# A tenth 2 MB weight buffer in shared rooms, with the norm rows spread by products of depth one

## What is computed

```
probs = softmax(h @ router_w + router_b)          # 32 experts in 8 groups of 4
expert, wts = the 2 best experts of the best group, per token
hid = silu(xt @ w_gate[e]) * (xt @ w_up[e])       # 1024 -> 512
y   = hid @ w_down[e]                             # 512 -> 1024
out = sum over the token's two experts of wts * y
x   = layer_norm(ALPHA * x + out, ln_g[i, 1], ln_b[i, 1])
```

## Time and profile before

| | |
|---|---|
| median of 3 runs | 1246.2 us (1245.13 to 1247.28) |
| profiled execution: span | 1245.5 us |
| TensorE busy | 1028.4 us, 83% of the span |
| VectorE, ScalarE, GpSimd busy | 24%, 15%, 3% |
| DMA | 451.10 MB, mean 362 GB/s |
| SP's queue | 442.51 MB, 86.0% of 16 engines |
| chain that ended last | TensorE 53%, DMA 43% |

### The profile page before, as it was taken

How to read it: one execution, slowest core, us unless ns; L and a number is a source line. 1 busy time by engine, 2 the same in 40 slices (tenths; PEclk the granted TensorE clock), 3 DMA queues, 4 the chain that set the end, 5 groups by cost and what they waited for, 6 DMA issues and landing times.

```text
span 1245.5 us, 18218 instructions
## 1 busy us (share of the span) xinstructions
PE 1028.4 (83%) x7608; PEld 572.4 (46%) x7608; DVE 293.8 (24%) x857; ACT 182.2 (15%) x466; POOL 42.7 (3%) x109
## 2 busy tenths in 40 slices
PE   7999999975688975568899899999866698855765
PEld 6675544442242442233588654544433343423432
DVE  0116431321111111111221685502111111111112
ACT  0014311100000000000221463211000010100002
POOL 3001010000000000000000120100000000000000
PEclk9999999988779988888999999999887799988798
DMA  9943589999999999999995305899999999999995
GB/s 329 396 170 147 223 349 419 428 427 427 428 426 428 426 428 427 427 427 424 381 328 205 134 1 203 314 423 425 426 427 428 428 427 428 428 426 428 426 427 216
DMA packets 55282, 451.10 MB, mean 362 GB/s; under 512 B 4363, under 2 KB 10764, under 8 KB 27548
## 3 DMA queue, kind: packets, MB, share of 16 engines
q1 hardware_dynamic: 52736, 442.51, 86.0%
q0 software_dynamic: 2128, 6.96, 1.6%
q10 hardware_dynamic: 332, 0.40, 0.1%
HBM read 448.78 MB, written 1.07 MB: 361 GB/s over the span
## 4 chain that ended last, share of the span: by engine, by line
PE 53%; DMA 43%; DVE 2%; ACT 1%; issue 1%; SPq 1%; DVEq 0%
PE bank L873 15%; DMA ring<-in_moe_w_up 14%; DMA ring<-in_moe_w_down 11%; PE bank L662 7%; DMA ring<-in_moe_w_gate 6%; DMA bias<-in_moe_w_gate 6%; DMA bias<-in_moe_w_up 5%; PE bank L737 5%; PE bank L840 4%; PE bank L935 3%; PE bank L913 2%; PE bank L669 2%; PE bank L950 2%; PE bank L1083 1%; PE bank L709 1%; PE bank L1152 1%
## 5 line engine op out<-in xcount | busy, mean ns | idle before, releaser
L873 PE MATMUL bank<-ring,work 128*32 128x256 f32 (+1 forms) x2624 | 351.9, 503 | 121.1 <-DMA ring<-in_moe_w_gate 43.5
L873 PEld LDWEIGHTS bank<-ring,work 128*32 128x32 f32 (+1 forms) x2624 | 160.8, 138 | 254.1 <-issue 230.2
L1456 DVE TENSOR_TENSOR work<-work,bank 128x256 f32<-128x256 f32 (+1 forms) x32 | 15.6, 488 | 550.4 <-PE bank L873 550.4
L873 PE MATMUL bank<-softmax_area,work 128*32 128x256 f32 (+1 forms) x416 | 78.5, 505 | 47.1 <-DMA ring<-in_moe_w_gate 27.1
L935 PE MATMUL bank<-ring,work 128*32 128x512 f32 x576 | 89.4, 601 | 12.6 <-DMA ring<-in_moe_w_down 6.8
L1464 DVE TENSOR_TENSOR xs<-xs,bank 128x512 f32<-128x512 f32 x120 | 76.6, 684 | 52.0 <-PE bank L950 27.0
L662 PE MATMUL bank<-xT,ring 128*128 128x256 f32 x384 | 85.0, 381 | 0.0
L662 PEld LDWEIGHTS bank<-xT,ring 128*128 128x128 f32 x384 | 72.3, 190 | 11.0 <-issue 1.4
L873 PEld LDWEIGHTS bank<-softmax_area,work 128*32 128x32 f32 (+1 forms) x416 | 36.1, 141 | 88.5 <-issue 81.3
L840 PE MATMUL bank<-work,acc 128*128 128x128 f32 (+1 forms) x448 | 75.1, 323 | 0.0
L840 PEld LDWEIGHTS bank<-work,acc 128*128 128x128 f32 x448 | 65.8, 191 | 15.1 <-issue 9.9
(11 more groups left out here) (245 smaller groups left out, 1041.5 us busy)
## 6 DMA issues: line engine op xcount, KB each, us to landing
ring<-in_moe_w_gate SPq DMA_DIRECT2D x44, 2048.0 KB, 30.3
ring<-in_moe_w_up SPq DMA_DIRECT2D x42, 2048.0 KB, 29.5
ring<-in_moe_w_down SPq DMA_DIRECT2D x36, 2048.0 KB, 29.8
ring<-in_moe_w_down SPq DMA_DIRECT2D x18, 1024.0 KB, 12.7
bias<-in_moe_w_down SPq DMA_DIRECT2D x8, 2048.0 KB, 32.5
softmax_area<-in_moe_w_down SPq DMA_DIRECT2D x8, 2048.0 KB, 22.1
bias<-in_moe_w_up SPq DMA_DIRECT2D x8, 2048.0 KB, 31.0
ring<-in_moe_w_gate SPq DMA_DIRECT2D x12, 1024.0 KB, 10.8
```

What stands on the lines that cost most here:

```text
L873: last = mm(bank[2 + k][row:row + cap, 0:width], xgT[:, t, at + e * cap:at + (e + 1) * cap], w[e](t)[:, part * width:(part + 1) * width], ...
```

## The change

- `gate_w`, `cmp_w2`, `pos_rows`, `cmp_hid`, `cmp_hidT`, `cmp_keyT`, `cmp_val` and `gates` become views of one tensor, `nsa_area`, 8 KB per partition.
- Pair 1's second up matrix, key (1, 3), gets a tenth buffer in halves: `nsa_area` and `norm_w`. Both keys (1, 2) and (1, 3) are now outside the planner's eight buffers.
- SP issues the halves of both spares between other loads, each after the wait that frees it.
- The compressed branch's five small loads are issued after layer 0's last down product (`load_nsa`) and counted by `nsa_loaded`; TensorE waits for them, and for `pads_ready` at 3, ahead of group 2 of layer 1.
- `load_norm` now runs twice, for the attention norms only. For the expert norms the two rows are loaded as four half rows on partitions 0, 32, 64 and 96 (`load_norm_rows`), and behind pairs 5, 6, 7 and 10 one half row each is multiplied by a row of ones into bank 2 (`spread_row`) and copied to `norm_w` by ScalarE.
- Six pairs of semaphores, one for each layer, become single ones that go on counting (`mix_ready`, `mix_added`, `order_ready`, `chosen_ready`, `ranks_ready`, `flag_ready`).

```diff
-SMALL_LOADS = 9 * 16
+SMALL_LOADS = 4 * 16
+NSA_LOADS = 5 * 16
...
+        nsa_area = sb("nsa_area", [P, SLOT // 2])
+        gate_w = nsa_area[:, 0:464]
...
+        gates = nsa_area[:, 1824:1920].rearrange("p (t n) -> p t n", t=NT)
+        norm_rows = nsa_area[:, 976:1488]
...
+        spare_parts = {SPARE_SLOTS[0]: [work[:, 0:2048], xT[:, :, :].rearrange("p t q -> p (t q)")],
+                       SPARE_SLOTS[1]: [nsa_area[:, :], norm_w[:, :, :].rearrange("p w d -> p (w d)")]}
+        def spare_of(key):
+            return {(1, 2): SPARE_SLOTS[0], (1, 3): SPARE_SLOTS[1]}.get(key[2:]) if key[0] == "pair" else None
...
+        ROW_PAIRS = (5, 6, 7, 10)
...
-                if slot_no(u) == SPARE_SLOT:
-                    sp.wait_ge(scores_read[l], len(job_pairs[l]))
-                    sp.dma_start(spare_parts[0]...)
-                    sp.wait_ge(logits_ready, l + 1)
-                    sp.dma_start(spare_parts[1]...)
-                    return
...
             def load_experts(l):
-                for i in range(FIXED // 2):
-                    for j in range(USES_PER_PAIR):
-                        load_use(l, i, j, (2 * i, 2 * i + 1))
-                sp.wait_ge(order_ready[l], 4)
+                for j in range(4):
+                    load_use(l, 0, j, (0, 1))
+                load_use(l, 0, 4, (0, 1))
+                sp.wait_ge(scores_read[l], len(job_pairs[l]))
+                load_spare(l, 2, 0)
+                load_use(l, 0, 5, (0, 1))
+                if l:
+                    sp.wait_ge(pv_done[l], len(job_pairs[l]))
+                load_spare(l, 3, 0)
+                for j in range(2):
+                    load_use(l, 1, j, (2, 3))
+                sp.wait_ge(normed_tiles, norm_tiles(l, 0, NT - 1))
+                load_spare(l, 3, 1)
+                sp.wait_ge(logits_ready, l + 1)
+                load_spare(l, 2, 1)
+                for j in range(4, USES_PER_PAIR):
+                    load_use(l, 1, j, (2, 3))
+                sp.wait_ge(order_ready, 4 * (l + 1))
...
+            def load_nsa():
+                pool.wait_ge(down_done[0], downs_through(PAIRS - 1))
+                nc.gpsimd.memset(gate_w[:, KT * 3 * HEADS:], 0.0).then_inc(pads_ready, 1)
+                pool.dma_start(gate_w[:, 0:KT * 3 * HEADS]..., nsa_w_in...).then_inc(nsa_loaded, 16)
+                for b, src in enumerate((nsa_pos_k, nsa_pos_v)):
+                    pool.dma_start(pos_rows[:, b, :], ...).then_inc(nsa_loaded, 16)
+                for b, src in enumerate((nsa_ck_w2, nsa_cv_w2)):
+                    pool.dma_start(cmp_w2[:, b, :, :], ...).then_inc(nsa_loaded, 16)
+            def load_norm_rows(l):
+                pool.wait_ge(up_done[l], 2)
+                for w, src in enumerate((ln_g, ln_b)):
+                    pool.dma_start(norm_rows[2 * 32 * w:2 * 32 * (w + 1):32, :],
+                                   bass.AP(tensor=src.tensor, offset=(2 * l + 1) * D, ap=[[512, 2], [1, 512]])).then_inc(rows_loaded, 16)
...
                 scale_probs(l)
-                load_norm(2 * l + 1)
                 order_columns(l)
+                load_norm_rows(l)
                 if l + 1 < LAYERS:
                     pool.wait_ge(logits_ready, l + 1)
                     pool.dma_start(router_t, ...).then_inc(small_loaded, 16)
-                    load_norm(2 * l + 2)
+                    load_nsa()
+                    load_norm(l + 1)
...
+            def spread_row(l, r):
+                if r == 0:
+                    pe.wait_ge(rows_loaded, 32 * (l + 1))
+                at = slice(32 * r, 32 * r + 1)
+                mm(bank[2][:, :], table("ones")[at, :], norm_rows[at, :], start=True, stop=True).then_inc(row_psum, 1)
+                pe.wait_ge(row_copied, len(ROW_PAIRS) * l + r + 1)
...
+                    if i in ROW_PAIRS:
+                        spread_row(l, ROW_PAIRS.index(i))
...
                 if g == 2:
                     proj_bank_free(1, g)
+                    pe.wait_ge(nsa_loaded, NSA_LOADS)
+                    pe.wait_ge(pads_ready, 3)
...
-                    dve.wait_ge(norm_loaded, 32 * (2 * l + 2))
+                    dve.wait_ge(row_copied, len(ROW_PAIRS) * (l + 1))
...
+                    if i in ROW_PAIRS:
+                        r = ROW_PAIRS.index(i)
+                        act.wait_ge(row_psum, len(ROW_PAIRS) * l + r + 1)
+                        s_.copy(norm_w[:, r // 2, r % 2 * 512:(r % 2 + 1) * 512], bank[2][:, :]).then_inc(row_copied, 1)
```

More of the change, by code:

```diff
@@ L120, in build @@
         router = sb("router", [P, (KT - 1) * E + P])
-        gate_w = sb("gate_w", [P, (KT - 1) * 3 * HEADS + P])
         router_bias = sb("router_bias", [P, E])
@@ L233, in build @@
         slot_views = [ring[:, s, :] for s in range(NSLOT)] + [softmax_area[:, :], bias[:, :, :].rearrange("p h k -> p (h k)")]
[L234 to L239 removed]
+        SOFTMAX_SLOT, BIAS_SLOT, SPARE_SLOTS = NSLOT, NSLOT + 1, (NSLOT + 2, NSLOT + 3)
+        spare_parts = {SPARE_SLOTS[0]: [work[:, 0:2048], xT[:, :, :].rearrange("p t q -> p (t q)")],
+                       SPARE_SLOTS[1]: [nsa_area[:, :], norm_w[:, :, :].rearrange("p w d -> p (w d)")]}
+        def spare_of(key):
+            return {(1, 2): SPARE_SLOTS[0], (1, 3): SPARE_SLOTS[1]}.get(key[2:]) if key[0] == "pair" else None
         def refill_cuts(key):
@@ L265, in share_slots @@
             slot, before, times = {}, {}, {}
-            loads = [-1] + [0] * (NSLOT + 2)
+            loads = [-1] + [0] * (NSLOT + 3)
             for l in range(LAYERS):
@@ L273, in share_slots @@
                         continue
-                    if in_spare(key):
-                        loads[SPARE_SLOT] += 2
-                        slot[key], before[key], times[key] = SPARE_SLOT, None, loads[SPARE_SLOT]
+                    if spare_of(key):
+                        s = spare_of(key)
+                        loads[s] += 2
+                        slot[key], before[key], times[key] = s, None, loads[s]
                         continue
@@ L301, in slot16 @@
             return slot_views[slot_no(u)].rearrange("p (t n) -> p t n", t=16)
-        loaded = [sem(f"loaded{s}") for s in range(NSLOT + 3)]
+        loaded = [sem(f"loaded{s}") for s in range(NSLOT + 4)]
         x_loaded, first_loaded = [sem(f"x_loaded{tt}") for tt in range(NT)], [sem(f"first_loaded{k}") for k in range(2)]
@@ L524, in load_use, with load_spare @@
                 sp.dma_start(dst, src).then_inc(loaded[slot_no(u)], 16)
-            def load_experts(l):
-                for i in range(FIXED // 2):
-                    for j in range(USES_PER_PAIR):
-                        load_use(l, i, j, (2 * i, 2 * i + 1))
-                sp.wait_ge(order_ready[l], 4)
+            def load_spare(l, j, half):
+                kind, e = PAIR_USES[j]
+                s = slot_no(ring_use["pair", l, 1, j])
+                at = slice(half * KT // 2, (half + 1) * KT // 2)
+                sp.dma_start(spare_parts[s][half].rearrange("p (t n) -> p t n", t=KT // 2),
+                             weights_of(l, kind, 2 + e)[:, at, :]).then_inc(loaded[s], 16)
+            def load_experts(l):
+                for j in range(4):
[16 more added lines that the diff above has]
+                sp.wait_ge(order_ready, 4 * (l + 1))
                 for i in range(FIXED // 2, PAIRS):
@@ L750, in out_piece @@
                 if m == KT - 1:
-                    last.then_inc(mix_ready[l], 1)
+                    last.then_inc(mix_ready, 1)
             def out_rest(l):
@@ L759, in out_rest @@
                         last = out_product(l, m, 1, n)
-                last.then_inc(mix_ready[l], 1)
-                pe.wait_ge(mix_added[l], 2)
+                last.then_inc(mix_ready, 1)
+                pe.wait_ge(mix_added, 4 * l + 2)
                 transpose_x(2 * l + 1, 0, acc)
```

92 lines of the change are left out of this document (42 added, 50 removed).

## The result

The changed kernel takes **1239.76 us** (median of 4 runs, 1238.35 to 1240.3), the kernel before 1246.1 us (4 runs, 1245.13 to 1247.28): ratio 0.9949, 95% interval 0.9937 to 0.996. The gain is 6.3 us where the forecast said 4.2. A second set of runs gave 1239.96 and 0.9955 (0.9941 to 0.9968).

A forecast was written before the change was run, and what follows sets the result against it. Expert phases were taken as bound by the DMA weight stream. Each layer's 4.91 us buffer gain, less its dry-queue gap, left 2.0 us; with 0.2 at the start, -4.2 us off the 1246.2 median gave 1242.0, range 1238.8 to 1246.4.

The forecast's parts named there:

- place of the dip: Weight queue runs dry in each expert phase before pair 1's downs free buffers: GB/s near 0 for about 3 us.
- what the dip gives back: Loss from the dry weight queue in each expert phase: 3.2 us in layer 0, 2.9 us in layer 1.
- restart of 1.93 us: Delay from SP's next issue after the dry queue until it runs as if at rate, taken from 164.52: 1.93 us.
- low bound by landings: Dry-queue gap in layer 0 read from when transfers land instead of bytes moved: only 1.3 us.
- short-gap rival: Dry queue restarts as landings have it, gap 1.3 us: gains 2 x 3.6 + 0.2, 1238.8 us; chance 0.12.
- The eaten buffer: Rival: refills after the dry queue come in small pieces and the loss reaches 4.9 us: 1246 us; chance 0.23.
- The late small loads: Rival: gate_w and the rest are served one after another, TensorE stands at the gate projection: 1253.2 us; chance 0.07.
- The router's 0.3 us: In layer 0 POOL's 128 KB router reload moves into the dry-queue gap, so 0.3 us comes back.
- The start's 0.2 us: At the program's start four small loads leave the queue shared with the first weights: gain 0.2 us, between 0 and 1.2.
- The norm rows at nothing: Norm-row steps behind pairs 5, 6, 7 and 10, 10 to 16 us of TensorE, cost nothing, covered by queued weights.
- The 0.7 us between span and median: Profiled span 1245.5 is 0.7 us under the median of 1246.2; the forecast takes its gain off the median.
- The page's 0.6 us to the first byte: Trainium skill's latency for SP's transfers, used as the dry queue's restart: gaps 1.9 and 1.6 us, 1239.4 us.

The follow-up runs named there:

- no_tenth: The changed kernel with key (1, 3) put back in the ring of planned buffers, all other parts of the change kept: 1246.12 us, ratio 0.9998.
- the drains: The changed kernel with SP waiting until its last issued transfer landed, ahead of pair 12's refills (1245.57 us) or those of pairs 6, 9 and 12 (1258.86 us).
- tenth_down: The changed kernel with the tenth buffer given to pair 1's first down matrix (1, 4) and (1, 3) back in the ring: 1237.96 us, ratio 0.9943.

## Why the prediction was right, and where it was off

**Bound, place of the dip: right; gross worth not measured by itself.** The phases end with DMA, the buffer is the only gain (no_tenth: nothing else clear of the noise), the 4.91 us are its bytes at the rate of the windows, SP has nothing to issue from pair 1's last refill to its downs, and the queue is dry once per layer. The forecast's 207 to 210 and 837 to 840, less the earlier starts of 1.8 and 5.6 us, are 205 to 208 and 831 to 834; the rows show 205 to 209 and 832 to 836. Nothing is dry afterwards, and line 526's landings from 240 to 560 us are 22.6/30.3/36.2, as in the earlier trace rows.

**The term that was mis-sized: what the dip gives back.** The prediction charged it in bytes, 3.2 and 2.9 us, and took the restart of 1.93 us from the byte count because "the end and the restart are then both counted in bytes". As a forecast of bytes this was near: 2.3 and 3.1 us are missing, 2.6 and 2.4 in the second profile. The restart was 1.6 to 1.9 us: issued at 206.50, the queue had moved by 209 as much as if it ran at full rate from about 208.1 to 208.4 on. But bytes were the wrong currency. The phases lost 4.91 - 3.3 = 1.6 and 4.91 - 3.4 = 1.5 us, next to the 1.3 that the prediction had as its low bound by landings and set aside since "landings mix in the next transfers' bytes". Not all missing bytes are lost time: about 1 us of them comes back at the end of layer 1's stream, 0.5 in the next stage's bytes of layer 0, and the drains, where 4.1 and 4.2 us of bytes are missing, cost 3.0 and 2.5. That the last engine's landings set the time is the reading that fits this; it wasn't seen directly. Landings aren't a sure price either: they said 1.8 and 0.6. So the mechanism was the forecast's, the size the short-gap rival's: 1239.76 lies 2.2 below the forecast, 0.96 above that rival's 1238.8.

**The eaten buffer** didn't come: with 1.5 us per dip, far from 4.9. **The late small loads** didn't either. The prediction bounded their landing at 18.5 us from a queue that was full of weights; at 597.84 the queue held what the next attention stage needs, and they took 5.8 to 6.5.

**The router's 0.3 us: not settled.** Its reload went out at 201.73 and was down 5.5 us later, at 207.2. POOL's queue moved 0.02, 0.08 and 0.04 MB in the rows of 204, 205 and 206, so most of it ran while SP's queue was falling dry, in part in time that nobody else used. No run moves it by itself, and 0.3 us is below the scatter of the phases. **The start's 0.2 us: not to be told** from the clock's scatter there. **The norm rows at nothing: right**, up to four times as many, but for a price that the prediction didn't look for, at the next stage's start: 0.55 us of standstill there in after, and 25.25 us to the gate projection where 24.4 were forecast. That the rows are its cause, and not the program's other changes, wasn't tested; no_tenth, which has them too, shows it, before doesn't.

**The 0.7 us between span and median** says nothing about the profiled execution of before: its own time is 1247.28, 1.8 above its span, as 1238.35 is above 1236.6 in after. The forecast was taken off the median, so nothing hung on it.

**The page's 0.6 us to the first byte.** The sum by it, 1239.4, is the nearest of all to the result, and for the wrong reason. The Trainium skill (DMA: Bandwidth & Descriptors, Latency and other measured facts) has about 0.6 us for a transfer issued by SP; after's queue took 1.6 to 1.9 us by the count above, a different quantity, since the rate comes up over some rows. The sum came out because a restart that is 1.3 too short makes up for a gap counted 1.5 too long.

**The best version.** tenth_down at 1237.96 us has the lowest median of all; but its ratio, 0.993 to 0.9957, overlaps after's 0.9941 to 0.9968 of the same set, and the 0.5 and 0.7 us per phase come from one profile. It may be better than after by 1 to 2 us; that isn't shown.

## What to carry to other kernels

One more buffer of prefetch is worth its bytes over the rate only if the order of releases feeds the queue behind it: list what the issuing engine may send after the phase's first release, add up the bytes, and look for the stretch that they don't cover; moving the buffer to another use only moves that stretch. Don't take all of the bytes that the windows miss as lost time, and look at the end of the stream for what comes back: here 2.3 to 3.1 us of missing bytes cost 1.5 to 1.6 us, and 4.1 to 4.2 us cost 2.5 to 3.0. Landings gave 1.8 and 0.6, nearer on average but not layer by layer. And compare stages between two events inside the trace: the phases repeated within 0.6 us, where whole spans of one kernel differed by 2.

## What was not expected of the hardware

A long stream over 16 DMA engines ends raggedly: the last transfers land over some 5 us at about half the rate and less, 197 GB/s and falling, and one that was dry some 120 us earlier ends within 3. Small loads on POOL's queue behind a phase's end land in 5.8 to 6.5 us. And 24 more steps of TensorE inside an expert phase, all hidden there, brought a standstill of 3.23 us with a granted clock of 0.57 behind it at the start of the next stage, 5 us in all. It ends 2.4 us after a packet of the queue called instruction; the cause stays inferred.
